# Dense weights' high halves: loaded from DRAM a second time and rounded on the way, instead of cast from the copy on chip

## What is computed

```
layer 0:  h += (u * (W_s v + b)) @ a_w_out        with u, v = gelu(norm(h) @ a_w_in)       # 1024 x 6144, 3072 x 1024
          h += (silu(a) * b) @ f_w_out            with a, b = norm(h) @ f_w_in             # 1024 x 5632, 2816 x 1024
layer 1:  k, v, f = norm(h) @ kv_w ; q, gate = norm(h) @ b_w_in ; forgetting attention     # 1024 x 2064, 1024 x 2048
          h += (attention * sigmoid(gate)) @ b_w_out                                       # 1024 x 1024
          h += top-2 of 8 SwiGLU experts (m_w_in, m_w_out)                                 # 8 x (1024 x 7168, 3584 x 1024)
layer 2:  attention and mLSTM on norm(h) @ w_in_2, then @ w_out_2                          # 1024 x 3080, 1024 x 1024
          h += norm(relu(norm(h) @ w_up_2)^2 @ w_down_2)                                   # 1024 x 4096, 4096 x 1024
```

## Time and profile before

| | us |
|---|---|
| median of 3 runs (2154.78 to 2159.66) | 2154.9 |
| the profiled execution | 2160.97 |
| its span, first to last instruction | 2159.3 |
| PE busy in it | 1998.0 (93%) |
| DVE busy | 1454.9 (67%) |
| ACT busy | 1188.7 (55%) |
| GpSimd busy | 2.3 (0%) |
| DMA, mean over the span | 233 GB/s (502.33 MB) |

### The profile page before, as it was taken

The page is one execution under the profiler, slowest core; times in us unless marked ns, Lnnn a source line. Parts: engine busy times, 40 slices in busy tenths (PEclk is TensorE's granted clock), DMA queues, the critical chain, the costliest instruction groups (busy, mean ns, idle before and its releaser), DMA issues.

```text
span 2159.3 us, 26236 instructions
## 1 busy us (share of the span) xinstructions
PE 1998.0 (93%) x9063; PEld 1647.8 (76%) x9063; DVE 1454.9 (67%) x1686; ACT 1188.7 (55%) x1246; POOL 2.3 (0%) x19
## 2 busy tenths in 40 slices
PE   3999899979898799999999999999999978977997
PEld 3998778868676688887888888788888857655886
DVE  2566345455553788889888888988888853546553
ACT  3444344435432577767777776767676734324532
POOL 0000000000000000000000000000000000000000
PEclk9999999989957799999999999999999988577999
DMA  5646545545405599999999999999999724023551
GB/s 166 201 163 215 175 141 191 177 135 175 137 1 170 177 368 352 346 366 331 366 332 369 348 346 365 332 366 333 371 347 345 279 88 156 0 67 113 180 177 39
DMA packets 352047, 502.33 MB, mean 233 GB/s; under 512 B 17576, under 2 KB 287980, under 8 KB 351980
## 3 DMA queue, kind: packets, MB, share of 16 engines
q1 hardware_dynamic: 346416, 498.65, 68.5%
q10 hardware_dynamic: 5564, 2.80, 0.5%
HBM read 500.35 MB, written 1.05 MB: 232 GB/s over the span
## 4 chain that ended last, share of the span: by engine, by line
PE 87%; DVE 7%; ACT 2%; issue 2%; ACTq 1%; DMA 0%; DVEq 0%
PE G L1055 21%; PE G L1057 21%; PE G L1056 21%; PE SM L1055 4%; PE SM L1056 4%; PE SM L1057 4%; PE T L1022 3%; PE G L1272 2%; PE G L1283 2%; PE SM L1240 1%; PE T L1301 1%; PE G L1224 1%; DVE work_r L1758 1%; DVE e_low L526 1%; PE SM L1049 1%
## 5 line engine op out<-in xcount | busy, mean ns | idle before, releaser
L526 DVE TENSOR_TENSOR e_low<-e_arrived,e_high 128x2048 fp32r<-128x2048 f32 x338 | 755.7, 2287 | 65.9 <-ACT e_high L521 65.4
L521 ACT CAST e_high<-e_arrived 128x2048 fp32r<-128x2048 f32 x338 | 624.3, 1912 | 0.1
L367 DVE TENSOR_TENSOR dense_low<-dense_raw,dense_high 128x2048 fp32r<-128x2048 f32 (+1 forms) x127 | 269.5, 2155 | 160.8 <-ACT dense_high L354 160.8
L1055 PE MATMUL G<-e_high,work_r 128*128 128x512 f32 x896 | 359.5, 401 | 4.7 <-DVE routing L1776 3.7
L1057 PE MATMUL G<-e_high,work_r 128*128 128x512 f32 x896 | 350.6, 391 | 0.0
L1056 PE MATMUL G<-e_low,work_r 128*128 128x512 f32 x896 | 349.8, 390 | 0.0
L1055 PE MATMUL G<-dense_high,xT_hi_all 128*128 128x512 f32 (+1 forms) x832 | 320.9, 386 | 11.0 <-DVE xT_lo_all L1477 7.5
L1056 PE MATMUL G<-dense_low,xT_hi_all 128*128 128x512 f32 (+1 forms) x832 | 315.6, 379 | 0.0
L1057 PE MATMUL G<-dense_high,xT_lo_all 128*128 128x512 f32 (+1 forms) x832 | 315.2, 379 | 0.0
L354 ACT CAST dense_high<-dense_raw 128x2048 fp32r<-128x2048 f32 (+1 forms) x127 | 223.4, 1799 | 96.3 <-PE G L1057 96.1
L1055 PEld LDWEIGHTS G<-e_high,work_r 128*128 128x128 f32 x896 | 169.0, 189 | 43.9 <-issue 5.8
(11 more groups left out here) (255 smaller groups left out, 2023.5 us busy)
## 6 DMA issues: line engine op xcount, KB each, us to landing
e_arrived<-in_m_w_in_dram SPq DMA_DIRECT2D x448, 512.0 KB, 5.5
e_arrived<-in_m_w_out_dram SPq DMA_DIRECT2D x224, 512.0 KB, 5.2
dense_raw<-in_a_w_in_dram SPq DMA_DIRECT2D x32, 768.0 KB, 5.0
dense_raw<-in_f_w_in_dram SPq DMA_DIRECT2D x44, 512.0 KB, 4.6
dense_raw<-in_w_up_dram SPq DMA_DIRECT2D x16, 1024.0 KB, 5.2
dense_raw<-in_w_down_dram SPq DMA_DIRECT2D x16, 1024.0 KB, 4.9
dense_raw<-in_a_w_out_dram SPq DMA_DIRECT2D x12, 1024.0 KB, 5.0
dense_raw<-in_f_w_out_dram SPq DMA_DIRECT2D x11, 1024.0 KB, 5.0
```

What stands on the lines that cost most here:

```text
L367: ins = nc.vector.tensor_tensor(unit_place(n, dense_low)[:, 0:w], unit_place(n, dense_raw)[:, 0:w], high_place(n)[:, 0:w].bitcast(F32), AL ...
L521: nc.scalar.copy(e_hi_unit(n), e_raw(n, e_arrived)).then_inc(e_hi, 1)
L526: nc.vector.tensor_tensor(e_raw(n, e_low), e_raw(n, e_arrived), e_hi_unit(n).bitcast(F32), ALU.subtract).then_inc(e_lo, 1)
L1055: nc.tensor.matmul(bank, x_hi, w_hi, start=start, stop=False)
```

## The change

The high half of a dense unit is no longer cast by ACT. GpSimd (the queue POOL) issues a second transfer of the same unit from DRAM, with fp32 as source and fp32r as destination, so that the transfer itself rounds; it goes straight to the unit's place in `dense_high`. This holds for all dense units but those of kv and qg, where a gain is folded in, and the two early ones of pr: for 127 units, 124.8 MB, in 149 transfers (fu's units take two). GpSimd waits for what ACT waited for, that PE is through with unit n - 4. The subtraction on DVE then waits for both landings, `dense_landed` and `high_landed`, in place of `dense_hi`.

```diff
+def cast_by_dma(n):
+
+    return not early(n) and not DENSE_FIRST["kv"] <= n < DENSE_FIRST["bo"]
+
+def high_count(n):
+    return 16 * sum(2 if DENSE_FIRST["fu"] <= m < DENSE_FIRST["fo"] else 1 for m in range(n + 1)
+                    if m % HIGH == n % HIGH and cast_by_dma(m))
+
+def scalar_count(n):
+    return sum(1 for m in range(n + 1) if not early(m) and not cast_by_dma(m))
...
+        high_landed = [sem(f"high_landed{j}") for j in range(HIGH)]
...
         def make_high(act, n):
 
+            if cast_by_dma(n):
+                return
             act.wait_ge(dense_landed[raw_slot(n)], landed_count(n))
...
         def make_low(dve, n):
 
-            dve.wait_ge(dense_hi, split_count(n))
+            if cast_by_dma(n):
+                dve.wait_ge(dense_landed[raw_slot(n)], landed_count(n))
+                dve.wait_ge(high_landed[n % HIGH], high_count(n))
+            else:
+                dve.wait_ge(dense_hi, scalar_count(n))
             w = 4 * phase_of(n).width
...
             ins.then_inc(consts_ready, 1)
+
+            def load_high(n):
+                ph = phase_of(n)
+                u = n - ph.first
+                half, s, w = u % 2, u // 2, ph.width
+                at, landed = high_place(n), high_landed[n % HIGH]
+                if ph.name in by_rows:
+                    pool.dma_start(at.rearrange("p (k n) -> p k n", k=2), by_rows[ph.name][u]).then_inc(landed, 16)
+                elif ph is fu:
+                    for b in range(2):
+                        pool.dma_start(at.rearrange("p (k b n) -> p k b n", k=4, b=2)[:, :, b, :],
+                                       f_in_pairs[:, 4 * half:4 * half + 4, b, s * PAIR:(s + 1) * PAIR]).then_inc(landed, 16)
+                else:
+                    src, shift = columns[ph.name]
+                    pool.dma_start(at[:, 0:4 * w].rearrange("p (k n) -> p k n", k=4),
+                                   src[:, 4 * half:4 * half + 4, shift + s * w:shift + (s + 1) * w]).then_inc(landed, 16)
+
+            for n in range(DENSE_ALL):
+                if not cast_by_dma(n):
+                    continue
+                if HIGH <= n < MOE_AFTER or n >= MOE_AFTER + EARLY + HIGH:
+                    consumed(pool, n - HIGH)
+                elif n >= MOE_AFTER:
+                    pool.wait_ge(last_scatter, 4)
+                load_high(n)
```

More of the change, by code:

```diff
@@ L549, in build @@
         block = ctx.enter_context(nc.Block())
+        f_in_pairs = t["f_w_in"][0].rearrange("(k p) (b n) -> p k b n", p=P, b=2)
+        columns = {"av": (a_in, A_HALF), "au": (a_in, 0), "kv": (kv_w, 0), "qg": (b_in, 0), "pr": (w_in2, 0), "mu": (w_up2, 0)}
+        by_rows = {"ao": a_out, "fo": f_out, "bo": b_out, "po": w_out2, "md": w_down2}
         @block.sync
         def _(sp):
-            f_in_pairs = t["f_w_in"][0].rearrange("(k p) (b n) -> p k b n", p=P, b=2)
-            columns = {"av": (a_in, A_HALF), "au": (a_in, 0), "kv": (kv_w, 0), "qg": (b_in, 0), "pr": (w_in2, 0), "mu": (w_up2, 0)}
-            by_rows = {"ao": a_out, "fo": f_out, "bo": b_out, "po": w_out2, "md": w_down2}
             def load(n):
```

## The result

| | before | after | ratio, 95% interval |
|---|---|---|---|
| median of the runs, us | 2157.0 (4 runs, 2154.8 to 2159.7) | 2196.1 (4 runs, 2186.3 to 2198.2) | 1.0172 [1.0137, 1.0207] |
| profiled execution, us | 2160.97 | 2197.96 | |
| its span, us | 2159.3 | 2196.2 | |

The changed kernel is 1.7% slower. The forecast was 2200, within 2161 to 2390. Of the experiments one run, of the kernel with six and six places, took 2347 us at a mean granted clock of 0.81 where all others had 0.92 to 0.94, and is left out of its median.

The account below looks back on a forecast made before the run. PE was taken to bound the dense phases, with DMA engines about half idle. Bandwidth costs of 51.7 us less credits of 15, plus 9.5 at the start, less 1.4, gave 44.8 us: 2200 us on the median, range 2161 to 2390.

Parts of the forecast that it names:

- start, with the cast's gain: Before the first product: four high units, 3.15 MB, compete with small transfers, +9.5 us; one removed cast gains 1.4 us.
- av, au: Dense phases: in av DMA engines take 4.77 us a unit against PE's 4.16, 16 units, 9.8 us; au nothing.
- ao: Dense phase ao: DMA engines take 5.79 us a unit against PE's 5.30, over 12 units, 5.9 us.
- fu, fo: Dense phases: fu 6.35 us a unit against 5.80, 22 units, 12.1 us; fo 5.79 against 5.28, seven units, 3.6.
- pr: Dense phase pr: DMA engines take 6.35 us a unit against PE's 5.44, over 10 units, 9.1 us.
- mu, md: Dense phases: mu 6.35 us a unit against 5.89, 16 units, 7.4 us; md 5.79 against 5.32, eight units, 3.8.
- the price of a unit: Where both streams run: a unit costs twice its bytes at 330 or 362 GB/s, less PE's time; 51.7 us summed.
- The credit of 3 us: Each of five phase groups starts with four high places full, which saves 3 us; 15 us in all.
- Issues: GpSimd issues 149 transfers, taken as 3 us a unit beside PE's work, only delaying a landing.
- The rival in which GpSimd's making binds: At 12 ns a row GpSimd's making of transfers bounds fu, av and au: 206 us more, 2361; chance 0.17.
- Rounding: Rival: rounding transfers cost the engines twice plain time, 360 us more, 2515, or one and a half times, 2352; chance 0.20.
- The hidden stream: Rival: two streams reach 401 to 410 GB/s, units stay under PE's time, only the start pays: +6.4 us, 2161; chance 0.12.

Follow-up runs that it names:

- six and six places: The changed kernel with its weight places divided into six raw and six high instead of eight and four, same bytes: 2168.1 us, ratio 1.0044.
- the profiled span of one run: The changed kernel with ScalarE again casting the first four units, GpSimd's transfers beginning with unit 4: 2180.3 us, ratio 1.0112.
- half the bytes: The changed kernel, each high transfer after the first uses of the places bringing half its rows, all waits kept: 2175.7 us, ratio 1.0078.

## Why the prediction was right, and where its steps were not

The time and the sign were right: 44.8 us were forecast on the profiled execution, 37.0 came. Part of the frame was right too: PE bounds the dense stages, ScalarE's time was free to lose, the new stream fills the engines, and the start pays. The price of what comes after the start was not, and that its total still fits is luck. By step:

| step | forecast | measured |
|---|---|---|
| start, with the cast's gain | +8.1 | +7.4 |
| av, au | +9.8 less 3 | +14.6, all of it from the seam on |
| ao | +5.9 less 3, in part refilled | +1.0 |
| fu, fo | +15.7 less 3 | +7.3, all in fu |
| kv, attention | 0 | +2.0 |
| pr | +9.1 less 3 | +3.3, and 1.9 around it |
| mu, md | +11.2 less 3 | -1.2 |

**The step that failed is the price of a unit: its bytes by a rate, less what PE takes.** First its size. I took 330 GB/s, and 362 for rows of 4 KB, from stretches of the start. Two streams reach 340 in fu, 372 for 4 us in au, and 395 to 412 in fo. The stretch that gave 330 was no measure of two weight streams: of its packets 836 were of 64 bytes, beside 825 of 1.5 KB. With the second stream the same four microseconds move 363, and the packets of 64 bytes are not among them. By 340, fu's 22 units cost (6.17 - 5.80) x 22 = 8.1 us, and 7.3 were lost; by 395, fo's 5.31 us against 5.28 cost nothing, and nothing was lost. With these rates the terms of av, ao, fu, fo and md, 35.2 us as forecast, come to about 10 in all (an estimate from the rates just named, ahead of the credits). **Then its kind.** av lost nothing and its seams much, and neither comes out of an average. What belongs there is a second sum, the time round a place: 0.7 us of issue, a landing of 9.6, 1.8 of subtraction, about 1 behind other work, the unit's own 4.2 us: 17.3 us by four places, 4.3 us a unit in av against PE's 4.2, and 18.2 / 4 = 4.6 in au against 5.1. So four places just hold in a steady stage, and give way at a seam, where nothing is left over to take in a unit that comes late; the lower clock behind each wait is on top, and stood in no term. The two errors had opposite signs: rates too low made the loss too large, and the missing sum for the places made it too small. That is why 44.8 lies near 37; the working doesn't earn it. With six high places the bytes are the same and the loss behind the start is nil, which the forecast's sum could not give.

**The credit of 3 us** was priced by the right ingredients (landing 10 us, measured 9.6 and 10.8; two subtractions) but as a thing given once to a group. It is the lead itself, and it decides: with two places more, at the same landings, all stages were whole.

**Issues.** I took 3 us for what measured 0.74. It entered the credit, 6 us less GpSimd's 3 for each of five groups; with 0.74 the credits are about 26 us instead of 15, and the forecast would have been 11 us lower, near 34. The rival in which GpSimd's making binds is out. The Trainium skill's rule from "SBUF — State Buffer", "Who interferes with whom", that the prediction weighed, can now be held against rows: 38 of the 149 issues lay beside a dense subtraction, and took 0.74 us in the median, as did the 111 others. That a tensor_tensor leaves the making of descriptors alone agrees with this trace.

**Rounding** does make the transfer slower, but by 15 ns on 159 for 4 KB, 9%, where its rival had a half or the whole. For rows of 1 KB it is more, 60 ns against the 46 of the kernel before, and there the plain packets beside them take 60 too. (Two sums of the prediction come out a little off, which moves nothing: the units at the doubled price add up to 353 us and not 357, and the whole sum at 341 GB/s in all phases is 42 us and not 45.) In fu the engines' share for each GB/s rose from 0.55 / 173 to 1.18 / 327, by 13%, of which the rounding's part is not shown. **The hidden stream** was given 0.12 and wanted 401 to 410 GB/s. It came true in the kernel with six and six places, at 340 in fu: not the rate was missing but the places. **The start** was right in its cause (the small transfers wait behind the new ones) and within 1 us in size.

**Landings.** That both streams' landings double, and not the new one's alone, is seen in the rows after. The Trainium skill, "DMA: Bandwidth & Descriptors", section "SWDGE vs HWDGE vs iDMA", has each DMA engine take its queues in turn; by that, two streams with the same packets slow each other alike, and the 9.2 and 10.8 us in fu roughly agree.

Open are the 1.2 us that mu gained, and the 6.6 us by which the profiled span of one run was shorter in bo and the experts. The 2.0 us of kv and the attention go with more high places and with half the bytes alike (182.3 to 182.6 us); through which wait was not followed.

## What to carry to other kernels

When a stream is added beside another, make two sums and not one: bytes by rate against the consumer's time, and the time round a buffer place (issue, landing under load, what follows it, the consumer) by the number of places. Take the landing under load: here it was up to twice its quiet value. And look for places that are left over elsewhere: here two raw places turned into high ones were worth 28 us. Work taken from an engine that held 2% of the chain was worth nothing here, though it was 218 us of busy time.

## What was not expected of the hardware

- A DMA transfer that rounds fp32 to fp32r moves at nearly the plain rate with rows of 4 KB: 174 ns against 159 for a packet. With two queues at work, 355 GB/s in ao, 395 to 412 in fo's rows of 4 KB. With rows of 1 KB it was 60 ns against the 46 of the kernel before, for the plain packets beside it too.
- A rate read in a stretch of full engines holds for its mix of packets: 330 GB/s at a share of 1.11 with 836 packets of 64 bytes among them, 363 at 1.18 in the same four microseconds with packets of 512 bytes and 1.5 KB.
- GpSimd made a transfer of 128 x 6 KB in 0.74 us and a plain one in 0.75, SyncE in 0.37; 97 units issued by GpSimd in place of SyncE cost no time that could be told (1.0011 [0.9998, 1.0024]).
- GpSimd's plain transfers moved rows of 1.5 KB in packets of 4608 bytes, SyncE's in packets of 1536.
